# Split order, halves and banks in a two-block transformer kernel: first norm by token halves, last output slabs by columns, slab splits and turned banks reordered

## The reference, cut to what matters

```python
# block 1
proj = rmsnorm(x, norm_mix_g) @ w_in
...
x = x + mixed @ w_out
h2 = rmsnorm(x, norm_ffn_g)
up = causal_depthwise_conv(h2 @ w_up, conv_w, conv_b)
gate, val = jnp.split(up, 2, axis=-1)
x = x + (jax.nn.silu(gate) * val) @ w_down
# block 2, two layers
mix = hybrid_mixer(x, w_in[l], ...)   # MLA heads and index-selected sparse heads
x = layer_norm(ALPHA * x + mix, ...)
x = layer_norm(ALPHA * x + grouped_moe(x, ...), ...)
```

## Time and profile before

| | |
|---|---|
| median of the runs | 1162.57 us (1161.79 to 1163.64) |
| profiled execution, its own time | 1158.68 us |
| its span | 1156.8 us, so 1.88 us lie around it |
| VectorE, ScalarE, GpSimd busy | 563.0, 419.6, 89.3 us |
| mean granted TensorE clock | 0.978 |
| data moved | 294.56 MB, 255 GB/s on average |

### The profile page before, as it was taken

How to read it: one execution, slowest core, us unless ns; L and a number is a source line. 1 busy time by engine, 2 the same in 40 slices (tenths; PEclk the granted TensorE clock), 3 DMA queues, 4 the chain that set the end, 5 groups by cost and what they waited for, 6 DMA issues and landing times.

```text
span 1156.8 us, 16062 instructions
## 1 busy us (share of the span) xinstructions
PE 1086.6 (94%) x6197; PEld 739.8 (64%) x6204; DVE 563.0 (49%) x1054; ACT 419.6 (36%) x750; POOL 89.3 (8%) x114
## 2 busy tenths in 40 slices
PE   8999998999999998898999999989889899999996
PEld 5898977899999787675344443358767644444332
DVE  5754375766666556756222222274684722222224
ACT  5355434545455345733111111143474311111111
POOL 1200000000000011520000000011152000000000
PEclk9999998999999999999999999999989999999997
DMA  8743253546555433339999999944241999999992
GB/s 291 262 146 110 87 190 125 181 152 213 181 174 188 140 118 122 111 121 388 421 420 419 420 420 420 417 150 126 75 152 68 365 393 420 419 419 420 420 420 104
DMA packets 81684, 294.56 MB, mean 255 GB/s; under 512 B 7252, under 2 KB 40386, under 8 KB 56914
## 3 DMA queue, kind: packets, MB, share of 16 engines
q1 hardware_dynamic: 79456, 289.29, 65.2%
q10 hardware_dynamic: 1394, 2.18, 0.5%
q0 software_dynamic: 768, 2.19, 0.5%
HBM read 292.59 MB, written 1.05 MB: 254 GB/s over the span
## 4 chain that ended last, share of the span: by engine, by line
PE 77%; DVE 9%; DMA 5%; ACT 5%; issue 3%; POOL 0%; SPq 0%; ACTq 0%; DVEq 0%
PE bank L2289 17%; PE bank L2298 8%; PE bank L1846 7%; PE bank L1847 7%; PE bank L1848 7%; PE bank L1901 4%; PE bank L1902 4%; PE bank L1903 4%; PE bank L1776 4%; PE bank L2276 3%; DMA raw<-in_w_in 3%; PE bank L2321 3%; PE bank L1935 2%; DMA k_t<-in_w_up 2%; PE bank L1919 2%
## 5 line engine op out<-in xcount | busy, mean ns | idle before, releaser
L1092 DVE TENSOR_TENSOR lo<-raw,hi 128x2048 fp32r<-128x2048 f32 (+3 forms) x79 | 168.4, 2149 | 70.3 <-ACT hi L688 70.0
L688 ACT CAST hi<-raw 128x2048 fp32r<-128x2048 f32 (+3 forms) x79 | 140.1, 1796 | 50.8 <-PE bank L1848 46.9
L1901 PE MATMUL bank<-xs,hi 128*128 128x256 f32 x448 | 128.8, 287 | 7.3 <-DVE lo L1092 3.5
L1321 DVE TENSOR_TENSOR proj<-bank,proj 64x512 f32<-64x512 f32 x32 | 34.6, 1082 | 205.2 <-PE bank L2311 192.8
L1846 PE MATMUL bank<-hi,xs 128*128 128x512 f32 (+2 forms) x312 | 124.2, 398 | 9.8 <-DVE gates L1586 5.5
L1902 PE MATMUL bank<-xs,hi 128*128 128x256 f32 x448 | 127.6, 285 | 0.0
L1903 PE MATMUL bank<-xs,lo 128*128 128x256 f32 x448 | 127.6, 285 | 0.0
L1847 PE MATMUL bank<-hi,xs 128*128 128x512 f32 (+2 forms) x312 | 118.2, 379 | 0.0
L1848 PE MATMUL bank<-lo,xs 128*128 128x512 f32 (+2 forms) x312 | 118.1, 379 | 0.0
L1030 ACT ACTIVATE proj<-bank 64x512 f32<-64x512 f32 x32 | 18.8, 589 | 203.5 <-PE bank L2290 203.5
L1901 PEld LDWEIGHTS bank<-xs,hi 128*128 128x128 f32 x448 | 86.8, 194 | 8.9 <-issue 4.4
(11 more groups left out here) (280 smaller groups left out, 2097.7 us busy)
## 6 DMA issues: line engine op xcount, KB each, us to landing
raw<-in_w_up SPq DMA_DIRECT2D x40, 1024.0 KB, 5.2
raw<-in_w_in SPq DMA_DIRECT2D x28, 1024.0 KB, 5.4
moe_w<-in_w_gate SPq DMA_DIRECT2D x24, 1024.0 KB, 16.0
moe_w<-in_w_up SPq DMA_DIRECT2D x24, 1024.0 KB, 17.5
moe_w<-in_w_down SPq DMA_DIRECT2D x24, 1024.0 KB, 16.2
raw<-in_w_down SPq DMA_DIRECT2D x19, 1024.0 KB, 5.7
raw<-in_w_gate SPq DMA_DIRECT2D x10, 1024.0 KB, 13.0
raw<-in_w_o SPq DMA_DIRECT2D x8, 1024.0 KB, 4.9
```

The lines of the kernel that those rows point to most:

```text
L688: nc.scalar.copy(high(n)[:, 0:size], raw[:, n % RING, 0:size]).then_inc(S["hi_done"], 1)
L1092: tt(low(n)[:, 0:size], raw[:, n % RING, 0:size], high(n)[:, 0:size].bitcast(F32), ALU.subtract).then_inc(S["lo_done"], 1)
L1901: mm(dst, wh[:, k, col], x_hi, start=k == 0, stop=False)
```

## The change

- First norm: each half of x has its own semaphore, and mean square and root go half by half. `busy(13)` becomes `busy(3)`, and TensorE turns half by half. Slab 0 is cast and subtracted in two parts of 1024.
- Last two slabs of `w_out`: half 1 runs first all products of the left 512 columns (`left_out`), then all of the right. The second norm's squares, scaling and signals go by 512 columns. Slab 24 is split before half 0 is added to x, slab 25's high part before `xs` is written.
- Feed-forward: in the first step, slab 27 is split between the gate's and the value's taps. In the loop a step splits slab n+2 at its start, n+3 after the gate's taps, and n+4 after the silu, which on VectorE is ahead of the low part of the activations. So the last step splits slab 57.
- Last `w_down` slab: half 1 by columns too, and its left columns are added to x before the right are done.
- Sparse input: the last two copies of turned groups are ahead of the split of the `w_uv` slab; TensorE waits for the copies at the first index score and not at the slab before it; queries and keys are turned into banks 0 to 3, and the wait for the value's copy and for the relus stands after them; VectorE copies the keys before it masks the scores.
- Experts: the last `out_split` is ahead of the next layer's slab split on VectorE.
- Some semaphores are merged.

```diff
+            for i in range(HALVES):
+                dve.wait_ge(S[f"x_in{i}"], 16)
+                mean_square([(i, 1, D)], EPS_RMS, 1)
...
-            busy(13, bank[1])
-            w.next("normed", HALVES)
-            fm_chunk = feature_major(DC, lambda c, half: xn[:, half, c * P:(c + 1) * P], ahead=8)
+            busy(3, bank[1])
+            fm_chunk = feature_major_by_half(lambda c, half: xn[:, half, c * P:(c + 1) * P], normed_half)
...
+            first = slice(0, SLAB // 2), slice(SLAB // 2, SLAB)
+            for part, name in zip(first, ("first_high", "hi_done")):
+                dve.wait_ge(S[name], 1)
+                ins = tt(low(S_QK)[:, part], raw[:, S_QK, part], high(S_QK)[:, part].bitcast(F32), ALU.subtract)
...
+                    ins.then_inc(S["half_out"], 1)
+                    for s, k in last:
+                        ins = chunk_products(s, k, 1, columns=0)
+                    ins.then_inc(S["left_out"], 1)
+                    for s, k in last:
+                        ins = chunk_products(s, k, 1, columns=1)
+                        if k == k_per - 1:
                             ins.then_inc(S["slab_used"], 1)
...
             def ffn_step(n, par, j, jj=None):
                 first = jj is None
-                split_lo(n + 1, jj, 6)
+                if first:
+                    split_lo(n + 1)
                 split_lo(n + 2, jj, 6)
                 for side, name in ((0, "g"), (1, "v")):
-                    if side and not first:
-                        split_lo(n + 3, jj, 6)
...
+                    if side == 0:
+                        split_lo(n + 3, jj, 6)
                 dve.wait_ge(S["silu_done"], j + 1)
                 dve.wait_ge(S["taps_v"], j * 2 + 2)
                 tt(y[:, 1, :, :], y[:, 0, :, :], y[:, 1, :, :], ALU.mult).then_inc(S["act_ready"], 1)
+                if not first:
+                    split_lo(n + 4, jj, 6)
                 dve.wait_ge(S["act_hi"], j + 1)
...
+                    if i == 0:
+                        w.next("copied_even", 3)
+                        w.next("copied_odd", 3)
...
-                    for src, to, copied in ((q_up, bank[4 + 2 * (i % 2)], "copied_q"),
-                                            (k_up, bank[5 + 2 * (i % 2)], "copied_k")):
+                    for src, to, copied in ((q_up, q_turned(i), "copied_q"), (k_up, k_turned(i), "copied_k")):
...
                 mapped(EXPERTS - 1)
+                out_split(EXPERTS - 1)
                 splits_to(split[0])
-                out_split(EXPERTS - 1)
```

More of the change, by code:

```diff
@@ L807, in _ @@
             first_params()
-            act.wait_ge(S["x_in"], 16 * HALVES)
-            squares([x[:, i, :] for i in range(HALVES)], lambda i: xn[:, i, :])
+            squares([x[:, i, :] for i in range(HALVES)], lambda i: xn[:, i, :],
+                    after=lambda i: act.wait_ge(S[f"x_in{i}"], 16))
             w.next("turned_params")
@@ L880, in _ @@
                 nc.scalar.copy(xs[:, 2 * i:2 * i + 2, 0:SEQ], mix[:, 2 * i:2 * i + 2, :]).then_inc(S["mixed_hi"], 1)
[L881 to L883 removed]
             splits_to(S_FFN)
+            for i in range(HALVES):
+                for c in range(2):
+                    w.next("x_updated")
+                    part = slice(512 * c, 512 * (c + 1))
+                    nc.scalar.activation(xn[:, i, part], x[:, i, part], ACT.Square,
+                                         accum_out=stat[:, 0, 2 * i + c:2 * i + c + 1]).then_inc(S["squares_summed"], 1)
+            splits_to(S_FFN + 1)
             feature_major(DC, lambda c: V_G2 + c)
@@ L1407, in _ @@
             w.next("params_copied")
-            splits_to(S_QK)
+            first = slice(0, SLAB // 2), slice(SLAB // 2, SLAB)
+            for part, name in zip(first, ("first_high", "hi_done")):
+                dve.wait_ge(S[name], 1)
+                ins = tt(low(S_QK)[:, part], raw[:, S_QK, part], high(S_QK)[:, part].bitcast(F32), ALU.subtract)
+            ins.then_inc(S["lo_done"], 1)
+            split[0] += 1
             feature_major(DC, lambda c: V_G1 + c)
@@ L1498, in _, with add_to_x @@
             mixed_low(3)
-            splits_to(S_OUT + 3)
-            def add_to_x(first, half):
+            splits_to(S_FFN)
+            def add_to_x(first, half, last):
                 for i in range(2):
+                    if half and i:
+                        wait_slab(dve, "slab_used", last)
+                    elif i == 0:
+                        w.next("left_out" if half else "half_out")
                     part = x[:, half, 512 * i:512 * (i + 1)]
```

127 lines of the change are left out of this document (67 added, 60 removed).

## The result

| | before | changed |
|---|---|---|
| median of four executions of each | 1163.11 us (1161.79 to 1164.21) | 1144.86 us (1143.16 to 1149.76) |
| ratio | | 0.9862, 95% interval 0.9824 to 0.9899 |
| profiled execution, its span | 1158.68, 1156.8 us | 1144.47, 1142.7 us |
| all executions of this study, mean | 1163.1 us (53 of them, 1157.25 to 1168.61) | 1145.7 us (9, 1143.07 to 1149.76) |

What follows compares the result with a forecast made beforehand. TensorE, busy 94% of the span, was taken as the bound, so time could come only from its idle or low-clock stretches. Terms of 12.75 us plus 1.0 for the clock gave 1162.57 - 13.75 = 1148.8 us, range 1145.0 to 1153.5.

Steps and rivals of the forecast that it cites:

- the forecast's own 1146.5 to 1151: Whole kernel: the range given to the main case, 1148.8 us, which had a chance of 0.60.
- One of its signs of being wrong: Whole kernel: loop step over 16.9 us, low clock in first 20 us, or longer experts with DMA waits over 1.33.
- Start, 0.8: First norm and slab 0: casting and subtracting in halves brings the first product at 14.3 instead of 15.10, 0.8 us.
- Second norm, 2.4: Second norm: slab 24 split in idle time, half 1 by columns; first product at 183.95 instead of 186.33, 2.4 us.
- First loop step, 2.8: First feed-forward step: slab 27 split between gate and value taps, so TensorE's 2.81 us stall goes, 2.8 us.
- Loop and end, 0.2: Feed-forward: loop moves cost nothing; at the end a new 1.3 us wait, yet turns start at 381.6, 0.2 us earlier.
- The rival of a slower loop: Feed-forward loop: a wait per step on VectorE; at 2 us per step the time is 1168.8; chance 0.02.
- Sparse input, 3.1 per layer: Sparse input: 2.4 us from earlier last copies plus 0.7 before the logits, 3.1 per layer, 6.2 for two.
- The second term: End of the sparse input: free banks let four key copies run back to back, masks behind; logits 0.7 us earlier.
- Last scatter, 0.35: Last scatter of the experts: layer 0's split in between goes, wait 1.72 instead of 2.08, 0.35 us.
- The clock, 1.0: Second norm and after feed-forward: one of two falls goes, some 1.6, less 0.6 for the start; net 1.0, bounds -2 to 4.
- the first rival: Start: clock falls there and the other falls stay; gain 11, time 1151.5; chance 0.15.

Runs made afterwards that it cites:

- the rerun: The changed kernel once more with nothing edited: 1146.89 us (1143.07 to 1148.23), ratio 0.9864 to the kernel before.
- the run with the activations first: Changed kernel with a loop step's third split moved behind the activations' high and low parts on both engines: 1146.64 us, ratio 0.9850.

## Why the prediction was right, and where it was wrong

The direction and the terms of the sum held; the forecast of 1148.8 was 2 to 4 us too long, and its larger errors, the sparse input's and the clock's, went the same way, so none hid another. The first median, 1144.86, lies 0.1 us under the range of 1145.0 to 1153.5, the rerun's 1146.89 inside it; of the forecast's own 1146.5 to 1151 the first is outside and the rerun just inside. One of its signs of being wrong came, the low clock in the first 20 us; the others did not (the step stayed at 16.9 us, no wait for the experts' weights is over 1.33).

- **Start, 0.8.** Right: 5.23 - 4.44 = 0.79 from cast to first product. The other 0.59 came of the slab's landing, which let the casts of the changed kernel and its variants begin between 9.17 and 9.94 us, and those of before at 9.87 and 10.04.
- **Second norm, 2.4.** Measured 2.30, with half 1's left half added while the right ran.
- **First loop step, 2.8.** Exact in idle time. What it cost beside it, a fall in two of three traces that have this stall, was missed: the prediction took the 2.81 us as a stretch that "brought no fall", from one trace.
- **Loop and end, 0.2.** 16.9 us per step, a new wait of 1.34 us, and 0.27 gained (2.39 - 1.34 - 0.78). That the wait was free because VectorE binds the end was in the chain of the prediction, and the run with the activations first shows it. The rival of a slower loop fell.
- **Sparse input, 3.1 per layer.** Measured 3.44 and 3.43 between traces with equal low time, as 2.4 and 1.03. The second term was 0.7, by a row of work on VectorE. In fact the logits wait for the key copies only, and these were paced by the turns, before and after. The free banks did not make the copies run back to back: in the earlier trace rows and in the changed kernel the last of them waits 0.18 us for its turn. What went is TensorE's own wait of 1.1 us for the value's copy, which the sum had not listed.
- **Last scatter, 0.35.** 0.41. In the same stage the experts were 0.60 us shorter, which is what their wait for weights varies by (188.3 to 189.0 us in other traces).
- **The clock, 1.0.** The step that failed, by its size. In the two profiles it is -0.42: the fall behind the feed-forward went (0.88), the one at the second norm became shorter, and one came at the start (1.60; the first rival, whose price was right and whose time of 1151.5 did not come). Over all executions it is some 4 us. The mean granted clock is 0.9712 over 49 executions of before and 0.9767 over the changed kernel's nine. With a fall at 0.50 the low time is 2 x (1 - clock) x span, so 67 and 53 us, 13.6 less. Within one kernel's executions each microsecond of low time goes with 0.30 us of time (115 executions of twelve kernels; 0.33 for before alone, 0.37 for the changed kernel alone), which makes an estimated 4.1 to 5.0 us. The means lie 17.4 us apart, and the 12.4 to 13.3 that are left fit the measured terms below. The prediction laid one profile of before beside the median of other executions. That profile had 51.3 us low, 16 under the mean of its kernel, so it showed few of the falls that could go.

With the terms as measured (0.79, 2.30, 2.81, 0.27, 6.87, 0.41) the sum is 13.45 where 12.75 stood, and with 4.1 for the clock 17.6.

How the clock's 4 us divide over places is known in part. In these traces falls go with idle stretches at four places: the second norm (8 of 9 without fillers, none of 3 with), the start (4 of 7, none of 5), the 2.81 us of the first loop step (2 of 3, none of 11), and the 2.4 us ahead of the turns behind the feed-forward (2 of 4, none of 10). Only at the two norms was TensorE's idle time filled and nothing else edited; at the other two the order of splits differs as well. At these four places the prices above make an estimated 0.65 - 0.9 + 1.1 + 0.4, some 1.2 us, near the 1.0 of the prediction (second norm: 2.0 us in the first trace of before against a mean of 1.35 in nine; start: 4/7 of 1.6; loop step: 2/3 of 1.6; turns: half of 0.88). The rest lies elsewhere and stays open.

The Trainium skill, "TensorE: Matmul & The Clock Gate", "Part 1: The HAM clock gate", says that how many of the first products run at the low clock differs from run to run of one kernel. Here it is so through the whole span, with 51.3 and 74.5 us low in the same kernel; a sum made against one profile has to carry that as a bound.

## What to carry to other kernels

An idle stretch of TensorE of 2.0 to 2.8 us costs itself and, at some places and in part of the executions, a stretch at half clock behind it (1.4 to 1.6 us where products are dense, 0.7 to 0.9 where other engines set the pace). At others it did not (one of six at the 2.76 us waits), so look in several traces before you price it. Cover what can't be removed with filler products into a free bank. A wait in front of work whose result another engine holds up anyway is worth nothing: look for what that engine has in its row. Where executions spread by the clock, compare stages between fixed rows in several traces, not medians of five, and compare the mean granted clock of all executions: one profile is one draw.

## What the runs showed of the hardware that was not expected

- Ahead of the last scatter low stretches lasted 3.4, 6.8 or 10.2 us in every trace, and one in each layer began where TensorE had been busy throughout: at 416.7 in the changed kernel, 5.3 us into 48 products of only 72 columns at the end of `w_in_2`'s, which start every 0.11 us. In all 14 traces and both layers a fall begins 3.3 to 5.8 us behind the first of these. Whether the narrow products are the cause was not tested, and fillers into idle time can't reach this fall. The changed kernel's timeline and windows:

```profile
411.43 0.20 PE L1880 MATMUL bank<-hi,xs 128*128 128x72 f32 x1
```

```profile
414.00:416.70 2.70, 2.70 (x26) 2.70 (x26) 0.83 (x2) 0.00 (x0) 0.00 (x0) 1.00 0.51 106
416.00:420.00 4.00, 4.00 (x24) 4.00 (x24) 1.82 (x7) 1.68 (x4) 1.78 (x7) 0.59 0.61 239
```

- The same low time costs by place: 1.6 us at the start, 1.37 in the feed-forward, 1.64 in the input products of block 2, 0.7 among the attention heads, and up to 1.4 behind the last scatter, where the whole tail of products went at half speed in the first trace of before (14.96 us) and at full speed in the changed kernel's (13.55).
- Taking 10 fillers out at the first norm won 0.34 us from cast to first product, which the weights' landing otherwise sets, and put the clock of the first products at risk (an estimated 0.9 us on average).
